# Wider strips for three projections, and another order at the ends of both mixers

## The reference, cut to what matters

```python
# first block
h = modulate(x, norm_w[0], mod[0,0], mod[0,1])            # rms norm, scale, shift
x = x + 0.5 * mod[0,2] * swiglu(h, w13[0], w2[0])
h = modulate(x, norm_w[1], mod[1,0], mod[1,1])
x = x + mod[1,2] * hybrid_mixer(h)                        # "mixer 1"
h = modulate(x, norm_w[2], mod[2,0], mod[2,1])
x = x + 0.5 * mod[2,2] * swiglu(h, w13[1], w2[1])
# hybrid_mixer: proj = h @ w_in -> c_q 256, c_kv 128, k_rope 32, conv_in, gates
#   merged = sum(gates * [attention, convolution] @ w_branch);  return merged @ w_out
# second block
z = rmsnorm(x) @ w_in_2                                   # qa 1024, ka 256, va 256, qb, kb, vb, gates
y_a, y_b = mixer_a(qa, ka, va) @ w_out_a, mixer_b(qb, kb, vb) @ w_out_b
x = x + (gate_a * y_a + gate_b * y_b) @ w_out_2           # end of "mixer 2"
x = x + square(relu(rmsnorm(x) @ w_ff1)) @ w_ff2
x = x + sigmoid(rmsnorm(x) @ w_ple_gate) * (p @ w_ple)
return rmsnorm(x)
```

## Time and profile before

| | before |
|---|---|
| median of 3 runs | 1023.25 us (1022.52 to 1025.52) |
| profiled execution | 1022.83 us |
| its span, first to last instruction | 1021.0 us |
| PE busy | 98% |
| DVE busy | 70% |
| ACT busy | 53% |
| chain that ended last | PE 89%, DVE 7%, ACT 2%, DMA 2%, issue 1% |
| granted TensorE clock, mean | 0.998 |

### The profile page before, as it was taken

How to read it: one execution, slowest core, us unless ns; L and a number is a source line. 1 busy time by engine, 2 the same in 40 slices (tenths; PEclk the granted TensorE clock), 3 DMA queues, 4 the chain that set the end, 5 groups by cost and what they waited for, 6 DMA issues and landing times.

```text
span 1021.0 us, 19724 instructions
## 1 busy us (share of the span) xinstructions
PE 1004.9 (98%) x8440; PEld 983.6 (96%) x8440; DVE 716.5 (70%) x1234; ACT 536.9 (53%) x903; POOL 36.2 (4%) x71
## 2 busy tenths in 40 slices
PE   8999999999999999999999999999999999999997
PEld 6999999999999999999999999999999999999997
DVE  3587888978687787867665779655567775555586
ACT  4454444456656455544444577555456464444553
POOL 0121000000000010000000000004000000000000
PEclk9999999999999999999999999999999999999999
DMA  9979978956646673777646357446257565656521
GB/s 336 369 248 352 332 284 318 322 170 227 197 124 200 229 243 111 270 244 249 221 153 207 123 170 230 138 125 182 67 176 233 180 231 184 200 175 203 166 83 42
DMA packets 144479, 212.26 MB, mean 208 GB/s; under 512 B 4275, under 2 KB 121383, under 8 KB 144392
## 3 DMA queue, kind: packets, MB, share of 16 engines
q1 hardware_dynamic: 140032, 198.66, 58.2%
q0 software_dynamic: 4096, 12.10, 3.9%
q10 hardware_dynamic: 264, 0.25, 0.1%
HBM read 209.88 MB, written 1.11 MB: 207 GB/s over the span
## 4 chain that ended last, share of the span: by engine, by line
PE 89%; DVE 7%; ACT 2%; DMA 2%; issue 1%; SPq 0%; DVEq 0%
PE PS L471 87%; DVE wlo L1836 3%; PE PS L479 2%; DMA SC<-in_w_ada_dram 1%; DVE W L1778 1%; ACT whi L1329 1%; DVE hl L1787 0%; DVE xT L1787 0%; DMA SC<-in_x_dram 0%; DVE W L1787 0%; DVE SS L1778 0%; ACT W L1316 0%; ACT SR L1321 0%; DVE SR L1778 0%; ACT SC L1321 0%
## 5 line engine op out<-in xcount | busy, mean ns | idle before, releaser
L1836 DVE TENSOR_TENSOR wlo<-raw,whi 128x1024 fp32r<-128x1024 f32 (+2 forms) x331 | 386.3, 1186 | 151.8 <-ACT whi L1329 151.2
L1329 ACT ACTIVATE whi<-raw 128x1024 fp32r<-128x1024 f32 (+2 forms) x331 | 331.9, 1022 | 159.6 <-PE PS L471 129.5
L471 PE MATMUL PS<-hh,whi 128*128 128x256 f32 (+1 forms) x1376 | 391.7, 285 | 0.0
L471 PE MATMUL PS<-hh,wlo 128*128 128x256 f32 (+1 forms) x1376 | 387.6, 282 | 0.0
L471 PE MATMUL PS<-hl,whi 128*128 128x256 f32 (+1 forms) x1376 | 386.8, 281 | 0.0
L471 PE MATMUL PS<-SR,whi 128*128 128x256 f32 (+1 forms) x1824 | 328.6, 282 | 3.1 <-DVE xT L1787 1.6
L471 PEld LDWEIGHTS PS<-SR,whi 128*128 128x128 f32 x1824 | 279.9, 188 | 5.9 <-DVE xT L1787 2.4
L471 PEld LDWEIGHTS PS<-hh,whi 128*128 128x128 f32 x1376 | 259.1, 189 | 3.1 <-issue 2.2
L471 PEld LDWEIGHTS PS<-hl,whi 128*128 128x128 f32 x1376 | 260.2, 189 | 0.4
L471 PEld LDWEIGHTS PS<-hh,wlo 128*128 128x128 f32 x1376 | 260.0, 189 | 0.0
L471 PE MATMUL PS<-SR,wlo 128*128 128x256 f32 (+1 forms) x912 | 256.8, 282 | 0.0
(11 more groups left out here) (188 smaller groups left out, 741.2 us busy)
## 6 DMA issues: line engine op xcount, KB each, us to landing
raw<-in_ffn_w_dram SPq DMA_DIRECT2D x60, 1024.0 KB, 6.9
raw<-in_w_in_dram SPq DMA_DIRECT2D x38, 1024.0 KB, 5.5
raw<-in_w_ff_dram SPq DMA_DIRECT2D x32, 1024.0 KB, 5.3
raw<-in_w_ada_dram SPq DMA_DIRECT2D x20, 1024.0 KB, 6.8
SC<-in_w_ada_dram SPq DMA_DIRECT2D x8, 1024.0 KB, 11.1
SC<-in_w_ada_dram POOLq DMA_DIRECT2D x8, 1024.0 KB, 7.7
raw<-in_w_out_dram SPq DMA_DIRECT2D x8, 1024.0 KB, 5.1
raw<-in_ffn_w_dram SPq DMA_DIRECT2D x7, 768.0 KB, 10.4
```

Source lines behind the costliest of these rows:

```text
L471: return e.matmul(o, l, r, start=start, stop=stop, skip_group_check=True)
L1329: e.activation(hi_part(p), raw_part(p), ACT.Copy).then_inc(*hi_done.up(p.i))
L1836: e.tensor_tensor(lo_part(p), raw_part(p), hi32(hi_part(p)), ALU.subtract).then_inc(*lo_done.up(p.i))
```

## The change

It has three parts. The numbering of lines moves by 1 for `mm` and by 17 for DVE's helpers.

1. The c strip is loaded and multiplied as one strip of 416 columns.
2. by_token has three pairs of 512 columns in place of six units of 256. The token sums stand inside the first pair, and `rstd_row` right behind it. DVE reads the sums (`token_mean`), then cuts the pieces of the first pair, then computes the root. ACT reads ka and va behind pair 1, and the last four heads of qa behind pair 2.
3. Ends of both mixers: DVE and ACT go through `finish_gated`. DVE adds all eight x, with only the first low parts between them. ACT takes the high parts and then squares all eight tiles, into six tiles of `W2f`, `SS` and `SQ`. PE begins the next stage with the 24 high by high matmuls (`three_high`), then the 48 others, and only then the token sums. `last_columns` moves from behind row 5 to between rows 4 and 5, and ACT's `last()`, which feeds it, ahead of `m_hi` 7.

```diff
+
+            def three_high(ps, key, outs, starts, n):
+                for k in range(KD):
+                    on.wait_ge(act_done, (("xhi", key), k))
+                    for i, p in enumerate(ps):
+                        mm(outs[i], hi_part(p)[:, k, :], hh[:, k, 0:n], k == 0 and i in starts, False)
+                for p in ps:
+                    on.wait_ge(lo_done, p.i)
 
             def keep_busy(n, b=1):
...
@@ -727,14 +740,13 @@
 
             on.wait_ge(dve_done, ("x", 0, 6), ("x", 0, 7))
             for k in range(KD):
-                if k % 4 == 0:
-                    c0, c1 = take("c0"), take("c1")
+                if k % 2 == 0:
+                    p = take("c")
                 on.wait_ge(dve_done, (("h", 1), k))
-                for p, w, o in ((c0, 256, 0), (c1, 160, 256)):
-                    for t in range(2):
-                        m = mm3(PS[:, 2 + t, o:o + w], hx_tokens(k, t), halves(p, k % 4), k == 0 and o == 0, k == 7)
-                    if k % 4 == 3:
-                        m.then_inc(*count(("used", p.i), *(["c_rows"] if k == 7 and o else [])))
+                for t in range(2):
+                    m = mm3(PS[:, 2 + t, 0:CONV0], hx_tokens(k, t), halves(p, k % 2), k == 0, k == 7)
+                if k % 2 == 1:
+                    m.then_inc(*count(("used", p.i), *(["c_rows"] if k == 7 else [])))
             for q in (2, 3):
                 pair_rows(7, q, 0)
...
@@ -862,8 +874,9 @@
                         if j == 7:
                             last_rows()
                         row(j - 3)
+                        if j == 7:
+                            last_columns()
                         row(j - 2)
-                last_columns()
                 todo = [(take(name), aring[r % 4]) for r in (6, 7)]
                 on.wait_ge(dve_done, ("m", key, 7))
...
@@ -900,18 +913,18 @@
                 row_step(p, aring[r % 6], r == 0, ("row", 1, r))
 
             on.wait_ge(dve_done, "xs2_shift")
-            ps = [take(n) for n in ("g1", "u1", "g1")]
+            ps = [take(n, hi_done) for n in ("g1", "u1", "g1")]
+            for i in range(3):
+                on.wait_ge(dve_done, ("gm", 1, 4 + i))
+            three_high(ps, 1, [PS[:, b, 0:S + 2] for b in (4, 5, 6)], (0, 1, 2), S + 2)
             for k in range(KD):
-                if k == 6:
-                    on.wait_ge(dve_done, ("x", 1, 4))
-                    token_sums(0, 1)
                 on.wait_ge(dve_done, (("xs1", 1), k))
                 for i, (p, b) in enumerate(zip(ps, (4, 5, 6))):
-                    if k == 0:
-                        on.wait_ge(dve_done, ("gm", 1, 4 + i))
-                    m = mm3(PS[:, b, 0:S + 2], halves(p, k), hx(k, S + 2), k == 0, k == KD - 1)
+                    m = mm_low(PS[:, b, 0:S + 2], halves(p, k), hx(k, S + 2), k == KD - 1)
                     if k == KD - 1:
                         m.then_inc(*count(("used", p.i), (("g", "u", "g")[i], 1, i // 2)))
+            on.wait_ge(dve_done, ("x", 1, 4))
+            token_sums(0, 1)
             on.wait_ge(dve_done, ("gm", 1, 7))
             scaled("u1", 7, ("u", 1, 1))
...
@@ -952,31 +965,26 @@
 
 
             def by_token(n, name):
-                b = unit_bank[n]
-                if n < 4:
-                    on.wait_ge(dve_done, *((("mod", 8), ("u_in", 1, 20), ("u_in", 1, 21)) if n < 2 else (("u_in", 1, 21),)))
-                else:
-                    on.wait_ge(act_done, ("by_token", n - 4))
                 for k in range(KD):
-                    if k % 4 == 0:
+                    if n == 0 and k == 4:
+                        on.wait_ge(dve_done, ("x", 2, 7))
+                        token_sums(3, 2, True)
+                    if k % 2 == 0:
                         p = take(name)
                     on.wait_ge(dve_done, (("xs1", 2), k))
                     for t in range(2):
-                        m = mm3(PS[:, b, 256 * t:256 * t + 256], hx_tokens(k, t), halves(p, k % 4), k == 0 and t == 0, k == 7)
-                    if k % 4 == 3:
-                        m.then_inc(*count(("used", p.i), *([("by_token", n)] if k == 7 else [])))
-
+                        m = mm3(PS[:, pair_bank[n] + t, :], hx_tokens(k, t), halves(p, k % 2), k == 0, k == 7)
+                    if k % 2 == 1:
+                        m.then_inc(*count(("used", p.i), *([("by_pair", n)] if k == 7 else [])))
+
+            on.wait_ge(dve_done, ("mod", 8), ("u_in", 1, 20))
             by_token(0, "qa")
+            on.wait_ge(dve_done, ("spread", 2))
+            rstd_row(3, ("rstd_row", 3))
             on.wait_ge(dve_done, ("u_in", 1, 21))
-            token_sums(4, 2, True)
-            by_token(1, "qa")
-            on.wait_ge(dve_done, ("spread", 2), ("x", 2, 7))
-            rstd_row(3, ("rstd_row", 3))
-            on.wait_ge(dve_done, ("mean", 2))
-            by_token(2, "ka")
-            by_token(3, "qa")
-            by_token(4, "qa")
-            by_token(5, "va")
+            by_token(1, "ka_va")
+            on.wait_ge(act_done, ("by_token", 0), ("by_token", 1))
+            by_token(2, "qa")
             on.wait_ge(dve_done, ("keys2", 0), ("keys2", 1), ("x", 2, 6))
             for t in range(2):
...
@@ -1121,17 +1129,18 @@
             def relu_tile(j, c):
                 column_tile(PS[:, 4 + j % 4, 256 * c:256 * c + 256], "ff1", c == 0, ("xs1", 3), ("f", j, c))
 
-            ps = [take("ff1") for _ in range(3)]
+            ps = [take("ff1", hi_done) for _ in range(3)]
             on.wait_ge(dve_done, ("gm", 3, 4), ("gm", 3, 5))
+            outs = [PS[:, 4 + i // 2, 256 * (i % 2):256 * (i % 2) + 256] for i in range(3)]
+            three_high(ps, 3, outs, (0, 2), S)
             for k in range(KD):
-                if k == 6:
-                    on.wait_ge(dve_done, ("gm", 3, 7))
-                    token_sums(7, 3)
                 on.wait_ge(dve_done, (("xs1", 3), k))
                 for i, p in enumerate(ps):
-                    m = mm3(PS[:, 4 + i // 2, 256 * (i % 2):256 * (i % 2) + 256], halves(p, k), hx(k), k == 0 and i % 2 == 0, k == KD - 1)
+                    m = mm_low(outs[i], halves(p, k), hx(k), k == KD - 1)
                     if k == KD - 1:
                         m.then_inc(*count(("used", p.i), ("f", i // 2, i % 2)))
+            on.wait_ge(dve_done, ("gm", 3, 7))
+            token_sums(7, 3)
             relu_tile(1, 1)
             on.wait_ge(dve_done, ("spread", 3), ("gm", 3, 6))
...
@@ -1355,6 +1364,15 @@
                 func(SQ[:, (n - 1) % 2, :] if n else SS[:, :], xT[:, n, :], ACT.Square, ("sq", key, n))
                 copy(to[:, n, 0:S], xT[:, n, :], (("xhi", key), n), scale=gain[:, n:n + 1])
 
+            def finish_gated(key, to, gain, *free):
+                for n in range(8):
+                    hi_before(("acc", key, n), 0 if n % 2 else 1)
+                    on.wait_ge(dve_done, ("x", key, n))
+                    copy(to[:, n, 0:S], xT[:, n, :], (("xhi", key), n), scale=gain[:, n:n + 1])
+                on.wait_ge(mm_done, *free)
+                for n in range(8):
+                    func(square_at[n], xT[:, n, :], ACT.Square, ("sq", key, n))
+
             def ada_rows_out(v, b, c, *pe_keys):
                 on.wait_ge(mm_done, *pe_keys)
...
@@ -1554,20 +1572,19 @@
                 for j in range(8):
                     hi_before(("stage", key, j))
                     opening(j)
+                    if j == 7 and last:
+                        last()
                     on.wait_ge(dve_done, ("mv", key, j))
                     if j >= 4:
                         on.wait_ge(mm_done, ("out_row", key, j - 4))
                     copy(aring[j % 4][0], W1[:, j % 3, 0:256], ("m_hi", key, j))
-                    if j == 7 and last:
-                        last()
                     hi_after(("stage", key, j))
 
             gated(1, lambda j: opened(j // 2 + 1, j // 2 + 5) if j % 2 and j < 7 else None, lambda: ada_rows_out(6, 4, 0, ("ada_sum", 6)))
             hi_before(("ada_col", 6), 2)
             on.wait_ge(dve_done, ("mod", 6))
             copy(hh[:, :, S:S + 2], mod[:, 6, :].unsqueeze(2).to_broadcast([128, KD, 2]), "xs2_shift")
-            for n in range(8):
-                finish(1, n, hh, mod[:, 7, :], ("sums", 0))
+            finish_gated(1, hh, mod[:, 7, :], ("sums", 0))
 
 
...
@@ -1957,6 +1974,30 @@
                     if n:
                         low_gained(key, n - 1, to, gain)
                 low_gained(key, 7, to, gain)
+
+            def finish_gated(key, gate, to, gain, next_key):
+                def low(n):
+                    after_act((("xhi", key), n), most=0)
+                    stt(to[1][:, n, 0:S], xT[:, n, :], gain[:, n:n + 1], hi32(to[0][:, n, 0:S]), ALU.mult, ALU.subtract, (("xs1", key), n))
+
+                last_one()
+                for n in range(8):
+                    lo_for(("acc", key, n), 1 if n in (4, 6) else 0)
+                    on.wait_ge(mm_done, ("acc", key, n))
+                    if gate is None:
```

(66 more changed lines are left out.)

## The result

| | before | changed |
|---|---|---|
| median | 1022.96 us (4 runs, 1022.52 to 1025.52) | 1033.99 us (4 runs, 1032.17 to 1036.67) |
| ratio | | 1.011, 95% interval 1.009 to 1.0129 |
| profiled execution | 1022.83 us | 1032.17 us |
| its span | 1021.0 us | 1030.3 us |
| PE busy | 1004.9 us | 1003.8 us |

Slower was forecast, by 5.75 us at the median; it is slower by 11.0. The waits came where they were expected, each within 0.4 us of the expected length. What the sum left out is TensorE's clock, which fell behind two of them. It was a rival, with a chance of 0.17.

A forecast was written before the change was run, and what follows sets the result against it. PE was taken to bound the kernel, busy 1004.9 of 1021.0 us. Terms -1.8 + 2.6 + 1.8 + 3.3 = +5.9, plus 2.25 from span to median, gave 1029.1, predicted as 1029 us, range 1021.5 to 1034.

The forecast's parts named there:

- c strip, -1.8: c strip: 48 matmuls of 416 columns replace 96, -2.1 us, less 0.2 to 0.3 lost on a low part.
- by_token, +2.6: by_token: wider matmuls and closed gaps win 0.7 and 0.9 us, but PE waits 4.2 us for the root behind pair 0.
- End of mixer 1, +1.8: End of mixer 1: PE waits 2.4 us for HT and 3.6 for the root; 1.5 won ahead is included.
- End of mixer 2, +3.3: End of mixer 2: gaps of 0.9 us close, but PE waits 4.4 us for the root behind six `wlo`.
- The clock, 0 in the sum: Rival, chance 0.17: PE's clock falls at the new waits; one or two falls give 1031 to 1034 us.
- the likeliest case: The forecast itself: three waits for the root without a fall of the clock, 1029 us, chance 0.55.
- The two signs of a wrong forecast: Idle ahead of the three `rstd_row` rows under 8 us together, or c strip matmuls starting slower than every 0.21 us.
- the sign of this rival: A slice of PE's clock below 1.00 would speak for the rival in which the clock falls, chance 0.17.
- The price in that rival: Clock rival, chance 0.17: 0 to 2.2 us more per fall, if the low clock lasts as long as the idle time.
- Only one wait bites: Rival, chance 0.18: one of three root waits absent, or all a third smaller; +1.5 to +2.6, 1024.7 to 1025.9 us.
- The rival on the other side: Rival, chance 0.10: the root isn't late at any of the three places, only gains stay, -5.8, 1017.4 us.

The follow-up runs named there:

- e6: Changed kernel with at most one (end of mixer 1) or two (by_token, end of mixer 2) `wlo` ahead of the root: 1018.63 us, ratio 0.9964.
- e9: Changed kernel with two `wlo` ahead of the root in place of six, at the end of mixer 2 alone: 1030.93 us, ratio 1.0091.
- e2: Kernel before with by_token alone in pairs of 512 columns: 1026.58 us, ratio 1.0045.
- e3: Kernel before with the two mixer ends alone changed: 1031.81 us, ratio 1.0086.
- e4: Changed kernel with 6, 8 and 9 calls of useless matmuls in the three waits for the root: 1032.15 us, ratio 1.0092.
- e5: Changed kernel with 13, 17 and 19 calls of useless matmuls in the root waits and 9 ahead of the HT transposes: 1028.82 us, ratio 1.0062.

## Why the prediction was half right

- **c strip, -1.8.** Measured -1.85 between the rows, -2.0 at the median alone. Right.
- **by_token, +2.6.** `rstd_row` was due at 597.25 and came at 597.01, with the whole stage 0.27 earlier; the wait was to be 4.2 and is 4.07. Without the clock the term is 4.1 - 1.6 = 2.5. Right. (Between 581.01 and 585.89 stand 36 matmuls, not the 40 that I counted; nothing in the sum hangs on that.)
- **End of mixer 1, +1.8.** HT 2.4 and the root 3.6 were forecast, 2.26 and 3.23 measured. DVE's five pieces ran from 392.77 without a pause, and the root was done somewhat sooner than my sum behind `whi` said. The rows moved by 1.86. Right.
- **End of mixer 2, +3.3.** Forecast 4.4 of wait, measured 4.53; 3.7 by the rows. Right, 0.4 short.
- **The clock, 0 in the sum.** This is the step that failed: the waits were counted at their length alone, and nothing for the slower matmuls behind them. I gave a fall 0.17 and called the likeliest case one without any. The argument against it was that the mean clock before is 0.998 and that no row shows a fall inside the program after any gap. But the longest gap behind a matmul in those rows was 1.62 us. They said nothing of 3.6 and 4.4 us, and the one long idle stretch that the trace did have, behind the last matmul, had ended in a fall. Measured: two falls in the profiled execution, 3.2 us, and 4.9 us at the median (the waits filled against the waits open). The two signs of a wrong forecast that I had given a number stayed silent: the idle time ahead of the three rows is 11.8 us, over the 8 asked for, and the strip's matmuls start every 0.19 us. Only the sign of this rival, a clock below 1.00, showed what was missing.
- **The price in that rival** was 0 to 2.2 us for each fall, and 1031 to 1034 in all for one or two. The median of 1033.99 lies at its upper edge, and two of the four runs lie above. That the size is about right is luck in part. I had supposed the clock to stay low for as long as PE had been idle, and it did not: it was low for the same 3.4 us behind waits of 2.25 (e6) and 4.53 us, and for 6 to 7 us behind 3.22 and 4.07 (e9). A short fall cost 1.1 to 1.6 us, a long one 2.2 and 2.6.
- **The chance of that rival** was far too small. Every open wait of over 4 us had a fall in its profile, five of five (two in the changed kernel, one each in e2, e3 and e9). The change has two such waits, so two falls were the likeliest case, and the shorter waits could add more.
- **Only one wait bites.** The upper bound of that rival doesn't follow from its own words: 5.9 less a stall of 3.6 is +2.3, not +2.6. No run showed this case, so nothing rests on it.
- **The rival on the other side.** That the order of the reads has a gain, if only the root isn't late, is shown too, but by kernels other than the changed one. 1017.4 was given for it, 5.8 us less than before. The root moved ahead gives 1018.63 with a fall at the wait for HT in its profile, and 1017.17, 5.5 us less than its own runs of before, once that wait is cut to half.

## What to carry to other kernels

Where an engine prepares work ahead in the gaps of another task, the event behind which it may prepare more is also a place in line. Here two to four more pieces came in ahead of the eleven to fifteen short instructions on which PE stood waiting. So for each wait of the bounding engine, list what the engine waited for does between the event that feeds it and the result, and move behind it everything that is not needed by then.

And where TensorE bounds the kernel, a wait has two prices, its length and the clock behind it. Where a wait is longer than any that the trace has shown to be harmless, the second has to be in the sum, with a chance for each wait.

## What the runs showed of the hardware

- Over all profiles, the granted clock fell at idle stretches of PE of 4.07 to 4.53 us in five cases of five, at 3.22 or 3.23 us in two of three, and at 2.24 to 2.51 us in four of seven. None was seen at 1.89 us (one case), nor at 1.62 us or less. These are stretches between matmuls, well inside the kernel. The clock fell between 1.2 us before and 1.5 us behind the first matmul after the wait, and stayed at 0.50 for about 3.4 us or for 6 to 7. The Trainium skill, "TensorE: Matmul & The Clock Gate", section "Part 1: The HAM clock gate (the "warmup" mystery)", says that an idle TensorE goes to 1.2 GHz, and the traces agree. The same section of the Trainium skill says that the number of matmuls at the lower clock at a kernel's start varies from run to run of one kernel. No run here was read for that; what varies in these traces is whether one and the same wait brings a fall.
- At the lower clock 512 columns start every 0.43 us and 256 every 0.21; at the higher 0.233 and 0.119. A fall of 3.4 us cost 1.1 to 1.6 us, one of 6 to 7 us 2.2 and 2.6.
- 416 columns start every 0.19 us at the higher clock.
- A wait filled by half with matmuls, and then 2.29 or 2.51 us idle, still led to a fall (e4). Filled up to the last 0.24 to 0.33 us, it did not (e5).
